# Dilated attention: three buffers for weight slices, scores left in PSUM until the exponential, output projection in eight chunks

## The chip, the cores and the metric

The kernel runs on one core of a Trainium2 chip. Five engines work from queues of their own and meet at semaphores: TensorE (PE) multiplies matrices and writes PSUM, VectorE (DVE) and ScalarE (ACT) do elementwise work and read and write PSUM and SBUF, GpSimd (POOL) works on SBUF alone, and SyncE (SP) issues most of the DMA transfers. SBUF is the working memory; PSUM has eight banks of 128 partitions by 512 fp32 values. The metric is the device time of one execution in microseconds (us), as the median of several runs.

## The reference, cut to what matters

Two layers work on 256 tokens of width 1024. Layer 0 has a pooling mixer, layer 1 the attention that is changed here; each is followed by a mixture of 64 experts. A condition vector `c` gives shift, scale and gate of every sub-layer through `ada_w`.

```
mod = silu(c) @ ada_w[i] + ada_b[i]                 # shift, scale, gate, twice
qkv = (h @ w_in).reshape(b, s, 3 groups, 3, 16 heads, 64)
for each group g (window, dilation) in ((128,1), (512,4), (2048,16)):
    sc = q @ k^T * 64**-0.5 - slope * distance      # only keys that are valid for g
    m = max(sc); p = exp(sc - m); den = sum(p)
    o_g = p @ v / den; lse_g = m + log(den)
mixed = sum_g softmax(lse)_g * o_g                  # (256, 16 heads * 64)
y = mixed @ w_out
x = layer_norm(ALPHA * x + (1 + g1) * y)            # then the experts of layer 1
```

The three groups of a head are the same as one softmax over all their keys together, and so the kernel computes them: 512 columns of scores (256 of group 0, 128 each of groups 1 and 2) for one query block.

## The kernel before

Everything is written out by hand for each engine in program order; there is no scheduler. The order of each engine's queue is the order of the Python code under `@block.sync`, `@block.scalar`, `@block.vector` and `@block.tensor`.

The attention layer is built like this:

- **Slices.** The input weight (1024 x 9216) arrives in 36 slices of 1 MB (`load_slice`), nine for each of four batches of heads; slices 36 to 39 are the output weight. To multiply fp32 data, each slice is split in two fp32r parts: ACT casts the high part (`slice_high`, line 780) and DVE subtracts it from the raw slice to get the low part (`slice_low`, line 445). Both parts lie in `slice_parts` (`wr`), which has two buffers. `project(n)` on PE is 48 matmuls of 256 columns (three products for each of 16 pieces, lines 1462 to 1464), and ACT copies its result out (`projected(n)`, line 808), then casts slice n+2.
- **Heads.** There are 16 steps that the code calls heads, `h` from 0 to 15, four to a batch (`HB`). One step is two real heads (index `j`) for one block of 128 queries. Per step: PE computes scores into banks 0 and 1 (`scores`, line 1525); DVE adds slope times distance, six instructions (line 1158), and takes the negative maximum, two (line 1163); ACT takes the exponential with its sum (line 824), DVE the reciprocal (line 1176), ACT multiplies (line 828); PE transposes the probabilities into banks 2 and 3 (line 1553); ACT and DVE copy one bank each to SBUF (`pT`, lines 832 and 1181); PE multiplies by the values (line 1564); DVE copies the 128 columns of result to `mixedT` (line 1192, `o_ready`).
- **What fills PE meanwhile.** `proj_of_head` puts projections of the next batch before and after the transposes of a step. The last batch has none; there `out_project(q)` for q = 0 to 3 (24 matmuls of 512 columns each) stands between the steps. It needs high and low parts of four heads' results, which ACT (`mixed_high`, line 814) and DVE (`mixed_low`, line 1169) make from `mixedT`.
- **Modulation.** The condition's matrix product runs beside this: DVE accumulates eight products for each 2 MB slice of `ada_w` (`gemv`, lines 865 and 867, in two halves, `part` 0 and 1), PE sums over partitions (`ada_sum`), DVE reads the sum (`ada_final`). Slices 16 to 23 belong here; they are loaded alternately into `slots0` ("S") and into units 6 and 7 of the weight memory.

Scores are biased from PSUM into the SBUF tile `sp_`, where the exponential also reads; so `scores(h+1)` waits on `s_read`, DVE's reading. DVE's list for a step begins with the reciprocal and the copy of `pT`, and only then has the bias and maximum of the next step.

Names for the text: S, T and V are the scores, transposes and value products on PE; P is one `project`.

Of the kernel before, what the change touches and what calls it, by code (L numbers as in the profile page):

```python
# [26 lines left out]
P = 128  # L27
# [12 lines left out]
HD = 64  # L40
# [88 lines left out]
def build(nc, a, out):  # L129
    ctx = ExitStack()  # L130
    with ctx:
# [106 lines left out]
        wr = in_weights("slice_parts", 0, [P, 2, 2, KD, BCOL], F32R)  # L238
# [11 lines left out]
        ada_place = [0, 2, 4, 6, "S", 0, 2, 4, 6, "S", "X", "S", 0, 2, 4, 6] + ["S", 6] * 4  # L250
# [17 lines left out]
        def sum_bank(n):  # L268

            return 5 if n >= 16 else (6, 7, 4, 5)[n - 12] if n >= 12 else 6 + n % 2  # L270
# [64 lines left out]
        s_mm, s_read, max_ready, p_exp, t_mm = sem("s_mm"), sem("s_read"), sem("max_ready"), sem("p_exp"), sem("p_T_mm")  # L335
# [36 lines left out]
        def proj_of_head(hb, hh):  # L372

            if hb == BATCHES - 1:
                return [], []
            before, after = [([0], [1]), ([2], [3]), ([4], [5]), ([6, 7], [8])][hh]
            return [9 * (hb + 1) + j for j in before], [9 * (hb + 1) + j for j in after]

# [4 lines left out]
        def gemv_of_head(hb, hh):  # L383

            return (18 + (hb * HB + hh) // 2, hh % 2) if hb < BATCHES - 1 else None

        def sum_of_head(hb, hh):

            return {(0, 1): 17, (0, 2): 18, (1, 0): 19, (1, 2): 20, (2, 0): 21, (2, 2): 22, (3, 0): 23}.get((hb, hh))
# [28 lines left out]

        def tokens_out(t, ks):

            return tmp[:, t, ks.start * P:ks.stop * P].rearrange("p (k r i) -> p k r i", k=4, r=4)
# [21 lines left out]
        def slice_lower(ops, n):  # L443

            ops.tensor_tensor(wr[:, n % 2, 1], slice_w(n), wr[:, n % 2, 0].bitcast(F32), ALU.subtract).then_inc(w_lo, 1)  # L445
# [3 lines left out]
        def _(sp):  # L449
# [96 lines left out]
            GEMV_LOADS = (12, 14, 17, 22, 26, 31)  # L546
# [21 lines left out]
            sp.wait_ge(ada_mm, 10)  # L568
            load_ada(17)
            for n in range(RAW, SLICES):  # L570
                if n in GEMV_LOADS:
                    m = 18 + GEMV_LOADS.index(n)
                    sp.wait_ge(ada_acc, m - 11)
                    load_ada(m)
                sp.wait_ge(w_lo, n - RAW + 1)
                load_slice(n)
# [87 lines left out]
        def _(act):  # L664
# [110 lines left out]
            def slice_high(n):  # L775
                if n < SLICES:
                    act.wait_ge(raw_in[n % RAW], 16 * (n // RAW + 1))
                    if n >= 2:
                        act.wait_ge(proj_mm, n - 1)
                    copy(wr[:, n % 2, 0], slice_w(n)).then_inc(w_hi, 1)  # L780
# [22 lines left out]
            slice_high(1)  # L803

            def projected(n):
# [4 lines left out]
                slice_high(n + 2)  # L810

            def mixed_high(b):

                copy(hThi[:, 2 * b:2 * b + 2], mixedT[:, 2 * b:2 * b + 2]).then_inc(hT_act, 1)

            for n in range(9):
                projected(n)
            for hb in range(BATCHES):
                for hh in range(HB):
                    h = hb * HB + hh  # L820
                    before, after = proj_of_head(hb, hh)
                    for j in range(2):
                        act.wait_ge(max_ready, 2 * h + j + 1)
                        nc.scalar.activation(sp_[:, j], sp_[:, j], ACT.Exp, bias=negmax[:, j:j + 1],
                                             accum_out=zsum[:, j:j + 1]).then_inc(p_exp, 1)
                    act.wait_ge(z_ready, h + 1)
                    for j in range(2):
                        nc.scalar.activation(sp_[:, j], sp_[:, j], ACT.Copy, scale=zinv[:, j:j + 1]).then_inc(p_ready, 1)
                    for n in before:
                        projected(n)  # L830
                    act.wait_ge(t_mm, h + 1)
                    copy(pT[:, 0], PS[:, 2, :]).then_inc(pT_act, 1)
                    if hb == BATCHES - 1 and hh < HB - 1:
                        mixed_high(hh)
                        if hh:
                            slice_high(9 * BATCHES + hh + 1)
                    for n in after:
                        projected(n)
            act.wait_ge(o_ready, HEADS)
            mixed_high(BATCHES - 1)  # L840
# [6 lines left out]
        def _(dve):  # L847
# [295 lines left out]
            for n in range(1, 11):  # L1143
                slice_low(n)
                if n in (6, 8):
                    gemv(16 + (n - 6) // 2, 0)
                if n in (7, 9):
                    gemv(16 + (n - 7) // 2, 1)
                if n == 10:
                    ada_final(16)  # L1150

            dve.wait_ge(dist_in, 16)
            def head_scores(h):
                hb, pair, it = place(h)
                dve.wait_ge(s_mm, h + 1)
                for j in range(2):
                    for g, (c0, c1) in enumerate(((0, 256), (256, 384), (384, 512))):
                        last = V.scalar_tensor_tensor(sp_[:, j, c0:c1], distT[:, it, c0:c1], -slope(g, hb * HB + 2 * pair + j),  # L1158
                                                      PS[:, j, c0:c1], ALU.mult, ALU.add)
                last.then_inc(s_read, 1)  # L1160
                dve.wait_ge(s_read, h + 1)
                for j in range(2):
                    V.tensor_reduce(negmax[:, j:j + 1], sp_[:, j], AX.X, ALU.max, negate=True).then_inc(max_ready, 1)
# [7 lines left out]
            head_scores(0)  # L1171
            for h in range(HEADS):
                hb, hh = h // HB, h % HB
                nxt = [n + 2 for part_of in proj_of_head(hb, hh) for n in part_of]
                dve.wait_ge(p_exp, 2 * (h + 1))
                V.reciprocal(zinv[:, :], zsum[:, :]).then_inc(z_ready, 1)
                early = nxt[:1] if hh == HB - 1 else []
                for n in early:
                    slice_low(n)
                dve.wait_ge(t_mm, h + 1)  # L1180
                copy(pT[:, 1], PS[:, 3, :]).then_inc(pT_dve, 1)
                if hh < HB - 1:
                    head_scores(h + 1)
                if (piece := gemv_of_head(hb, hh)) is not None:
                    gemv(*piece)
                if (n := sum_of_head(hb, hh)) is not None:
                    ada_final(n)
                for n in nxt[len(early):1]:
                    slice_low(n)
                dve.wait_ge(o_mm, h + 1)  # L1190
                _, pair, it = place(h)
                last = copy(in_order(mixedT, 2 * hb + pair)[:, 2 * it:2 * it + 2], PS[:, 2, 0:P].rearrange("p (r i) -> p r i", r=2))
                last.then_inc(o_ready, 1)
                for n in nxt[1:]:
                    if n < 9 * BATCHES:
                        slice_low(n)
                if hb == BATCHES - 1:
                    mixed_low(hh)
                    if hh < HB - 1:
                        slice_low(9 * BATCHES + hh + 1)  # L1200
                elif hh == HB - 1:
                    head_scores(h + 1)
                    if hb == BATCHES - 2:
                        slice_low(9 * BATCHES)
# [7 lines left out]
        def _(pe):  # L1212
# [105 lines left out]
            def moe(L):  # L1318
# [8 lines left out]
                pe.wait_ge(hT_act, (4, 14)[L])  # L1327
                pe.wait_ge(hT_dve, (4, 14)[L])
# [137 lines left out]
            def project(n):  # L1466
# [9 lines left out]
                w = wr[:, n % 2]  # L1476
# [11 lines left out]
            def out_project(q):  # L1488

# [145 lines left out]
```

## Time and profile before

| | |
|---|---|
| median of 3 runs | 1536.61 us (1533.97 to 1537.8) |
| profiled execution, its own time | 1533.0 us |
| its span, first to last instruction | 1531.2 us |
| mean granted TensorE clock | 0.976 of full |
| busy: PE / DVE / ACT / POOL | 1436.8 / 570.4 / 405.5 / 65.0 us |

The span has five parts: layer 0 with its experts (to about 630 us), the first nine projections (647.8 to 704.95), the 16 head steps (to 981.8, where the last output slice starts), norm and routing (to 1035.8), and the experts of layer 1. The profile's page gives busy shares over the whole span; the head steps are under a fifth of it, so what they wait for is read from views of that stretch alone. In a view of waits, "PE psum L1462 <- DVE slice_parts L445" means that PE stood idle before the instruction at line 1462 until the instruction of DVE at line 445 had ended. The granted clock is a share of full speed; 1.00 is 2.4 GHz, 0.50 is 1.2 GHz.

### The profile page before, as it was taken

The numbers are of one execution on the slowest core, as the hardware profiler recorded it, in microseconds if no ns is written. First come the engines' busy times: TensorE is split into PE (matmuls) and PEld (weight loads), VectorE is DVE, ScalarE is ACT, GpSimd is POOL, SyncE is SP. The second block draws the span as 40 slices with busy tenths as digits, with TensorE's granted clock in tenths as the row PEclk, the third lists the DMA queues.
The fourth block names the chain that finished last, engine by engine and source line by source line (L and its number), as shares of the span: only waits on it lengthen the run. The fifth ranks groups of instructions, "written<-read, shape, count | busy, mean of one in ns | idle before, by whom it ended". The sixth has DMA issues, their size and how long they took to land.

```text
span 1531.2 us, 19331 instructions
## 1 busy us (share of the span) xinstructions
PE 1436.8 (94%) x7546; PEld 818.7 (53%) x7546; DVE 570.4 (37%) x1108; ACT 405.5 (26%) x629; POOL 65.0 (4%) x46
## 2 busy tenths in 40 slices
PE   6999999999999999899888888689999999999994
PEld 3544444444444444498888887544444444444442
DVE  0574222222222222648566665551222222222225
ACT  1222112121221212435444444331212122121212
POOL 0001300000000000030000000022000000000001
PEclk9999999999999999899999999889999999999998
DMA  9994899999999999966444431367999999999990
GB/s 394 423 427 190 357 420 424 426 427 424 428 425 428 426 425 428 409 223 249 170 161 184 176 141 49 144 248 318 424 424 428 424 429 425 425 427 425 429 409 29
DMA packets 50512, 522.17 MB, mean 341 GB/s; under 512 B 5632, under 2 KB 5888, under 8 KB 8224
## 3 DMA queue, kind: packets, MB, share of 16 engines
q1 hardware_dynamic: 48512, 514.61, 80.9%
q0 software_dynamic: 1952, 6.88, 1.3%
q8 instruction: 34, 0.56, 0.1%
q14 instruction: 14, 0.11, 0.0%
HBM read 520.42 MB, written 1.05 MB: 341 GB/s over the span
## 4 chain that ended last, share of the span: by engine, by line
PE 87%; DVE 9%; DMA 2%; ACT 1%; issue 1%; SPq 0%; DVEq 0%; ACTq 0%
PE psum L1411 29%; PE psum L1436 15%; PE psum L1359 9%; PE psum L1368 9%; PE psum L1462 4%; PE psum L1463 4%; PE psum L1464 4%; PE psum L1267 2%; PE psum L1345 2%; PE psum L1312 2%; DVE slice_parts L445 2%; DVE modulation_sums L867 1%; DVE scores L1158 1%; PE psum L1553 1%; PE psum L1423 1%
## 5 line engine op out<-in xcount | busy, mean ns | idle before, releaser
L1411 PE MATMUL psum<-weights,slots_of_tokens 128*64 128x512 f32 x2048 | 450.4, 592 | 0.0
L1411 PEld LDWEIGHTS psum<-weights,slots_of_tokens 128*64 128x64 f32 x2048 | 146.9, 137 | 292.7 <-issue 292.7
L1436 PE MATMUL psum<-weights,hidden_T 128*64 128x512 f32 x1024 | 233.8, 598 | 0.0
L1112 DVE SCALAR_TENSOR_TENSOR slot_rows<-psum,slot_weight,slot_rows 128x512 fp32r<-128x512 f32 x128 | 96.1, 751 | 193.8 <-ACT slot_rows L770 193.8
L1098 DVE TENSOR_TENSOR hidden<-gate,psum 128x256 f32<-128x256 f32 x64 | 27.0, 421 | 374.8 <-ACT gate L762 374.8
L1359 PE MATMUL psum<-slot_matrix,h_parts 128*128 128x512 f32 x576 | 157.4, 399 | 0.0
L1368 PE MATMUL psum<-slot_rows,slots_T 128*128 128x512 f32 x528 | 140.5, 408 | 3.7 <-DVE slot_rows L1112 3.7
L1436 PEld LDWEIGHTS psum<-weights,hidden_T 128*64 128x64 f32 x1024 | 67.8, 136 | 132.8 <-issue 132.8
L1368 PEld LDWEIGHTS psum<-slot_rows,slots_T 128*128 128x128 f32 x528 | 94.6, 189 | 74.8 <-issue 57.3
L1462 PE MATMUL psum<-h_transposed_high,slice_parts 128*128 128x256 f32 x384 | 112.4, 293 | 23.0 <-DVE slice_parts L445 17.3
L762 ACT ACTIVATE gate<-psum 128x256 f32<-128x256 f32 x64 | 24.6, 384 | 410.2 <-PE psum L1411 410.2
L770 ACT ACTIVATE slot_rows<-psum,slot_weight 128x512 fp32r<-128x512 f32 x128 | 87.9, 687 | 136.3 <-PE psum L1436 136.3
L1359 PEld LDWEIGHTS psum<-slot_matrix,h_parts 128*128 128x128 f32 x576 | 103.6, 189 | 19.2 <-issue 1.0
L1463 PE MATMUL psum<-h_transposed_low,slice_parts 128*128 128x256 f32 x384 | 111.2, 290 | 0.0
L1464 PE MATMUL psum<-h_transposed_high,slice_parts 128*128 128x256 f32 x384 | 111.1, 289 | 0.0
L445 DVE TENSOR_TENSOR slice_parts<-weights,slice_parts 128x2048 fp32r<-128x2048 f32 x40 | 93.6, 2344 | 42.8 <-ACT slice_parts L780 42.7
L1462 PEld LDWEIGHTS psum<-h_transposed_high,slice_parts 128*128 128x128 f32 x384 | 76.3, 199 | 25.3 <-issue 24.3
L1100 DVE CAST slots_T<-psum 128x256 fp32r<-128x256 f32 x64 | 27.2, 425 | 161.3 <-PE psum L1425 161.3
L1462 PE MATMUL psum<-slice_parts,h_transposed_high 128*128 128x256 f32 (+1 forms) x224 | 69.2, 309 | 12.4 <-DVE slice_parts L445 6.4
L1464 PEld LDWEIGHTS psum<-h_transposed_high,slice_parts 128*128 128x128 f32 x384 | 76.3, 199 | 0.0
L1463 PEld LDWEIGHTS psum<-h_transposed_low,slice_parts 128*128 128x128 f32 x384 | 76.2, 198 | 0.0
L780 ACT CAST slice_parts<-weights 128x2048 fp32r<-128x2048 f32 x40 | 75.8, 1894 | 0.0
(182 smaller groups left out, 1386.6 us busy)
## 6 DMA issues: line engine op xcount, KB each, us to landing
weights<-in_exp_w_gu SPq DMA_DIRECT2D x128, 2048.0 KB, 15.6
weights<-in_exp_w_down SPq DMA_DIRECT2D x128, 1024.0 KB, 14.6
weights<-in_attn_w_in SPq DMA_DIRECT2D x36, 1024.0 KB, 6.1
weights<-in_ada_w SPq DMA_DIRECT2D x16, 2048.0 KB, 16.7
slots_of_tokens<-in_ada_w SPq DMA_DIRECT2D x7, 2048.0 KB, 13.0
weights<-in_pool_w_in SPq DMA_DIRECT2D x2, 2048.0 KB, 25.7
weights<-in_pool_w_out SPq DMA_DIRECT2D x2, 2048.0 KB, 20.5
weights<-in_sh_w_gu SPq DMA_DIRECT2D x2, 2048.0 KB, 10.1
```

The costliest lines, as they stand in the source:

```text
L445: ops.tensor_tensor(wr[:, n % 2, 1], slice_w(n), wr[:, n % 2, 0].bitcast(F32), ALU.subtract).then_inc(w_lo, 1)
L770: nc.scalar.activation(yw[:, 0, half * HALF:(half + 1) * HALF], PS[:, BD + half, :], ACT.Copy, scale=wslot[:, 0:1]).then_inc(lo.yh, 1)
L780: copy(wr[:, n % 2, 0], slice_w(n)).then_inc(w_hi, 1)
L1112: V.scalar_tensor_tensor(yw[:, 1, c], PS[:, BD + half, :], wslot[:, 0:1], yw[:, 0, c].bitcast(F32), ALU.mult, ALU.subtract).then_inc(lo.yl, 1)
L1267: last = mm(PS[:, u_bank(half, t), :], hT[:, k, t * P:(t + 1) * P], w_in[part][:, k - 4 * part, half * HALF:(half + 1) * HALF], start=k == ...
L1359: last = mm(PS[:, bank, :], hfs[:, s, t, k, :], Pm[b][:, t, :], start=s == 0 and t == 0, stop=s == 1 and t == TT - 1)
L1368: last = mm(PS[:, 2 * t + half, :], PT[:, t * P:(t + 1) * P], yw[:, s, half * HALF:(half + 1) * HALF], start=False, stop=True, skip_group_ ...
L1411: last = mm(PS[j * SLOTS:(j + 1) * SLOTS, BGU, :], XgT[ob][:, k, s0:s0 + SLOTS], gu_w(ws + j)[:, k, :], start=k == 0, stop=k == KD - 1, ti ...
L1436: last = mm(PS[j * SLOTS:(j + 1) * SLOTS, BD + half, :], HT[:, k, j * SLOTS:(j + 1) * SLOTS], dn_w(ws + j)[:, k, half * HALF:(half + 1) * ...
L1462: mm(out, *parts(0, 0), start=first, stop=False)
L1463: mm(out, *parts(1, 0), start=False, stop=False)
L1464: return mm(out, *parts(0, 1), start=False, stop=last)
```

## The change

- `slice_parts` gets a third buffer, in units 6 and 7. ACT casts slice n+3 after projection n, not n+2. Slices 0 to 2 are prepared ahead of the first projection.
- All modulation slices 16 to 23 are now loaded into `slots0`, each when the one before has been used (`GEMV_LOADS`, `ada_place`). Two of them, not one, are finished in the first nine projections; the others stand at the end of DVE's list of steps 0 to 9, then at steps 10 and 11. The last sum uses bank 3.
- DVE adds the bias in place, in PSUM, and takes the maximum there; the exponential reads PSUM and writes `sp_`. `scores(h+1)` now waits on `p_exp`, until ACT has read the scores of step h.
- DVE's list of a step begins with the bias and maximum of step h+1 (`head_scores(h + 1)`), ahead of the copy of `pT`; ACT's softmax of step h+1 stands behind its `pT` copy of step h and ahead of its `projected(after)`. At steps 3 and 7 (`scores_late`) the next step's scores come at the end, since they need the last projection.
- The projections of the last batch end at step 10 (three a step in steps 8 to 10), and `out_project` is cut in eight chunks of 12 matmuls: two each at steps 11, 12 and 13, one at 14, the last behind step 15.
- In steps 12 to 15 ACT and DVE write the high and low parts straight from PSUM, without `mixedT`.

```diff
-        wr = in_weights("slice_parts", 0, [P, 2, 2, KD, BCOL], F32R)
+        wr = [in_weights(f"slice_parts{i}", u0, [P, 2, KD, BCOL], F32R) for i, u0 in enumerate((0, 2, 6))]
-        ada_place = [0, 2, 4, 6, "S", 0, 2, 4, 6, "S", "X", "S", 0, 2, 4, 6] + ["S", 6] * 4
+        ada_place = [0, 2, 4, 6, "S", 0, 2, 4, 6, "S", "X", "S", 0, 2, 4, 6] + ["S"] * 8
+        def out_of_head(h):
+            return {HEADS - 5: (0, 1), HEADS - 4: (2, 3), HEADS - 3: (4, 5), HEADS - 2: (6,)}.get(h, ())
+        def sum_of_head(h):
+            return 17 + h // 2 if h % 2 == 0 and 2 <= h <= 10 else None
-            GEMV_LOADS = (12, 14, 17, 22, 26, 31)
+            GEMV_LOADS = (9, 13, 19, 24, 28, 33, 39)
...
@@ ACT @@
-                    for j in range(2):
-                        act.wait_ge(max_ready, 2 * h + j + 1)
-                        nc.scalar.activation(sp_[:, j], sp_[:, j], ACT.Exp, bias=negmax[:, j:j + 1],
...
+            softmax(0)
+            for h in range(HEADS):
+                for n in before:
+                    projected(n)
+                act.wait_ge(t_mm, h + 1)
+                copy(pT[:, 0], PS[:, 2, :]).then_inc(pT_act, 1)
+                if h < HEADS - 1 and not scores_late(h):
+                    softmax(h + 1)
+                for n in after:
+                    projected(n)
+                if scores_late(h):
+                    softmax(h + 1)
+                if h == HEADS - HB - 1:
+                    mixed_high(BATCHES - 2)
+                if h >= HEADS - HB:
+                    act.wait_ge(o_mm, h + 1)
+                    copy(o_in(hThi, h), o_out()).then_inc(hT_act, 1)
...
@@ DVE @@
-                        last = V.scalar_tensor_tensor(sp_[:, j, c0:c1], distT[:, it, c0:c1], -slope(g, hb * HB + 2 * pair + j),
+                        last = V.scalar_tensor_tensor(PS[:, j, c0:c1], distT[:, it, c0:c1], -slope(g, hb * HB + 2 * pair + j),
                                                       PS[:, j, c0:c1], ALU.mult, ALU.add)
-                    V.tensor_reduce(negmax[:, j:j + 1], sp_[:, j], AX.X, ALU.max, negate=True).then_inc(max_ready, 1)
+                    V.tensor_reduce(negmax[:, j:j + 1], PS[:, j, :], AX.X, ALU.max, negate=True).then_inc(max_ready, 1)
...
+                if early:
+                    head_scores(h + 1)
+                if (n := sum_of_head(h)) is not None:
+                    ada_final(n)
                 dve.wait_ge(t_mm, h + 1)
                 copy(pT[:, 1], PS[:, 3, :]).then_inc(pT_dve, 1)
+                if early:
+                    softmax_inverse(h + 1)
+                for n in before:
+                    slice_low(n + 3)
+                if h == HEADS - HB - 1:
+                    gemv(*gemv_of_head(h))
...
+                for n in after:
+                    slice_low(n + 3)
+                if gemv_of_head(h) is not None and h != HEADS - HB - 1:
+                    gemv(*gemv_of_head(h))
...
@@ PE @@
-                    pe.wait_ge(s_read, h)
+                    pe.wait_ge(p_exp, 2 * h)
```

**Place 1, DVE, step 1.** In these rows of the order `scores`/`psum` with `distances` is the bias, `slice_parts` the low part of a slice, `modulation_sums` a gemv half. Before:

```order
L1181 COPY probabilities_T<-psum 128x512
L1158 SCALAR_TENSOR_TENSOR scores<-distances,psum 128x256
L1158 SCALAR_TENSOR_TENSOR scores<-distances,psum 128x128 x2
L1158 SCALAR_TENSOR_TENSOR scores<-distances,psum 128x256
L1158 SCALAR_TENSOR_TENSOR scores<-distances,psum 128x128 x2
L1163 TENSOR_REDUCE negative_maximum<-scores 128x1 x2
L867 SCALAR_TENSOR_TENSOR modulation_sums<-slots_of_tokens,condition_silu,modulation_sums 128x512 x4
L884 SCALAR_TENSOR_TENSOR gates<-psum,gates 128x512
L445 TENSOR_TENSOR slice_parts<-weights,slice_parts 128x2048
L1192 COPY mixed_heads_T<-psum 128x2x64
L445 TENSOR_TENSOR slice_parts<-weights,slice_parts 128x2048
```

After, from the bias of step 2 to the end of the list of step 1:

```order
L1190 SCALAR_TENSOR_TENSOR psum<-distances,psum 128x256
L1190 SCALAR_TENSOR_TENSOR psum<-distances,psum 128x128 x2
L1190 SCALAR_TENSOR_TENSOR psum<-distances,psum 128x256
L1190 SCALAR_TENSOR_TENSOR psum<-distances,psum 128x128 x2
L1195 TENSOR_REDUCE negative_maximum<-psum 128x1 x2
L1218 COPY probabilities_T<-psum 128x512
L1200 RECIPROCAL softmax_inverse<-softmax_sum 128x2
L466 TENSOR_TENSOR slice_parts_82<-weights,slice_parts_82 128x2048
L1229 COPY mixed_heads_T<-psum 128x2x64
L466 TENSOR_TENSOR slice_parts_80<-weights,slice_parts_80 128x2048
L898 SCALAR_TENSOR_TENSOR modulation_sums<-slots_of_tokens,condition_silu,modulation_sums 128x512 x4
```

The bias and maximum have moved ahead of the `probabilities_T` copy, and the gemv half from the middle of the list to its end, behind both slices; PE's `ada_sum` of step 2 waits for that half.

**Place 2, DVE, where the output projection begins.** Before, step 12, which has no gemv:

```order
L1181 COPY probabilities_T<-psum 128x512
L1158 SCALAR_TENSOR_TENSOR scores<-distances,psum 128x256
L1158 SCALAR_TENSOR_TENSOR scores<-distances,psum 128x128 x2
L1158 SCALAR_TENSOR_TENSOR scores<-distances,psum 128x256
L1158 SCALAR_TENSOR_TENSOR scores<-distances,psum 128x128 x2
L1163 TENSOR_REDUCE negative_maximum<-scores 128x1 x2
L884 SCALAR_TENSOR_TENSOR gates<-psum,gates 128x512
L1192 COPY mixed_heads_T<-psum 128x2x64
L1169 TENSOR_TENSOR h_transposed_low<-mixed_heads_T,h_transposed_high 128x512
L445 TENSOR_TENSOR slice_parts<-weights,slice_parts 128x2048
```

After, the end of step 10 and most of step 11:

```order
L1206 TENSOR_TENSOR h_transposed_low<-mixed_heads_T,h_transposed_high 128x512 x2
L466 TENSOR_TENSOR slice_parts_82<-weights,slice_parts_82 128x2048
L896 TENSOR_SCALAR modulation_sums<-slots_of_tokens,condition_silu 128x512
L898 SCALAR_TENSOR_TENSOR modulation_sums<-slots_of_tokens,condition_silu,modulation_sums 128x512 x3
L1190 SCALAR_TENSOR_TENSOR psum<-distances,psum 128x256
L1190 SCALAR_TENSOR_TENSOR psum<-distances,psum 128x128 x2
L1190 SCALAR_TENSOR_TENSOR psum<-distances,psum 128x256
L1190 SCALAR_TENSOR_TENSOR psum<-distances,psum 128x128 x2
L1195 TENSOR_REDUCE negative_maximum<-psum 128x1 x2
L1218 COPY probabilities_T<-psum 128x512
L1200 RECIPROCAL softmax_inverse<-softmax_sum 128x2
L898 SCALAR_TENSOR_TENSOR modulation_sums<-slots_of_tokens,condition_silu,modulation_sums 128x512 x4
```

Both halves of the last gemv now stand here, the first ahead of the bias of step 12, the second ahead of the copy to `mixed_heads_T`.

**Place 3, PE, the end of the attention.** Before, the end of output slice 2, then step 15, then slice 3:

```order
L1463 MATMUL psum<-slice_parts,h_transposed_low 128x512
L1464 MATMUL psum<-slice_parts,h_transposed_high 128x512
L1553 MATMUL psum<-constants,scores 128x128 x8
L1564 MATMUL psum<-probabilities_T,qkv 64x128 x8
L1462 MATMUL psum<-slice_parts,h_transposed_high 128x512
L1463 MATMUL psum<-slice_parts,h_transposed_low 128x512
L1464 MATMUL psum<-slice_parts,h_transposed_high 128x512
L1462 MATMUL psum<-slice_parts,h_transposed_high 128x512
```

After, the end of chunk 6, the last `ada_sum`, V of step 14, then step 15 and chunk 7:

```order
L1505 MATMUL psum<-slice_parts_80,h_transposed_low 128x512
L1506 MATMUL psum<-slice_parts_80,h_transposed_high 128x512
L1278 MATMUL psum<-modulation_sums,constants 128x512
L1611 MATMUL psum<-probabilities_T,qkv 64x128 x8
L1594 MATMUL psum<-constants,scores 128x128 x8
L1611 MATMUL psum<-probabilities_T,qkv 64x128 x8
L1504 MATMUL psum<-slice_parts_80,h_transposed_high 128x512
L1505 MATMUL psum<-slice_parts_80,h_transposed_low 128x512
L1506 MATMUL psum<-slice_parts_80,h_transposed_high 128x512
```

The last sum stands between chunk 6 and V of step 14, and behind step 15 come 12 matmuls where there were 24.

## Rows read from the trace of the kernel before

**Rows 1.** The page: the chain that ended last, shares by engine.
```profile
PE 87%; DVE 9%; DMA 2%; ACT 1%; issue 1%; SPq 0%; DVEq 0%; ACTq 0%
```

**Rows 2.** Stretches: us from start, length, busy us of each engine, granted clock, DMA.
```profile
core 0: us, PE busy (x) PEld busy (x) DVE busy (x) ACT busy (x) POOL busy (x), PEclk, DMA share, GB/s
714.45:926.70 212.25, 188.61 (x1622) 181.32 (x1622) 129.81 (x202) 95.65 (x128) 0.00 (x0) 0.98 0.42 160
926.70:981.80 55.10, 41.45 (x283) 33.90 (x282) 30.98 (x59) 24.80 (x39) 0.54 (x1) 0.91 0.07 22
```

**Rows 3.** Waits from 714.4 to 981.8 us: total, times, longest.
```profile
PE psum L1462 <- DVE slice_parts L445: 23.6, 11, 2.7
...
PE psum L1462 <- DVE h_transposed_low L1169: 6.0, 4, 2.5
...
PE psum L1564 <- DVE probabilities_T L1181: 3.5, 4, 0.9
...
PE psum L1553 <- ACT scores L828: 3.3, 1, 3.3
```

**Rows 4.** Chain of waits through step 5: start us, length, instruction.
```profile
809.95 1.08 PE psum L1525 x12
811.03 1.04 PE psum L1553 x8
812.09 0.69 DVE probabilities_T L1181
812.78 1.46 DVE scores L1158 x6
814.27 1.28 DVE negative_maximum L1163 x2
815.55 0.67 DVE modulation_sums L867
...
818.57 2.21 DVE slice_parts L445
...
820.92 0.36 PE psum L1462
...
826.91 0.78 PE psum L1239 x8
```

**Rows 5.** Groups by line, 714.4 to 981.8 us: busy us, mean ns.
```profile
L780 ACT CAST slice_parts<-weights 128x2048 fp32r<-128x2048 f32 x29 | 54.9, 1893 | 0.0
...
L824 ACT ACTIVATE scores<-scores,negative_maximum 128x512 f32<-128x512 f32 x30 | 21.4, 715 | 15.0 <-DVE negative_maximum L1163 15.0
...
L1192 DVE COPY mixed_heads_T<-psum 128x128 f32<-128x128 f32 x16 | 6.2, 387 | 10.5 <-PE psum L1564 10.5
```

**Rows 6.** DMA issues into the block slots_of_tokens, 660 to 960 us.
```profile
DMA to landing us min/median/max: 7.9/7.9/8.8
```

**Rows 7.** Chain of waits from the second output slice to the next norm.
```profile
947.61 0.47 PE psum L1462
...
953.31 0.89 PE psum L1553 x8
...
977.90 0.70 DVE probabilities_T L1181
...
978.74 1.11 PE psum L1564 x16
...
980.28 0.63 ACT h_transposed_high L814
...
980.93 0.70 DVE h_transposed_low L1169
...
981.77 0.47 PE psum L1462
...
983.53 0.71 DVE psum L936
...
984.27 0.70 DVE residual_or_h L938
```

More of the change, by code:

```diff
@@ L1142, in _ @@
                     V.tensor_tensor(tokens_in(hTlo, ks, t), tokens_out(t, ks), tokens_in(hThi, ks, t).bitcast(F32), ALU.subtract).then_inc(hT_dve, 1)
-            for n in range(1, 11):
+            for n in range(1, 12):
                 slice_low(n)
[L1145 to L1149, printed above, removed]
+                if n in (3, 4):
+                    gemv(16, n - 3)
+                if n == 7:
                     ada_final(16)
+                if n in (7, 8):
+                    gemv(17, n - 7)
+            ada_final(17)
             dve.wait_ge(dist_in, 16)
@@ L1171, in _ @@
             head_scores(0)
+            softmax_inverse(0)
             for h in range(HEADS):
[L1173 to L1179, printed above, removed]
+                before, after = proj_of_head(h)
+                early = h < HEADS - 1 and not scores_late(h)
+                if early:
+                    head_scores(h + 1)
+                if (n := sum_of_head(h)) is not None:
+                    ada_final(n)
@@ L1192, in _ @@
[L1192 to L1204, printed above, removed]
+                if early:
+                    softmax_inverse(h + 1)
@@ L1569, in _ @@
-            out_project(BATCHES - 1)
+            for h in range(HEADS):
+                hb, pair, it = place(h)
+                before, after = proj_of_head(h)
+                for n in before:
+                    project(n)
+                n = sum_of_head(h)
+                if n is not None:
+                    ada_sum(n)
+                if h < HEADS - 1 and not scores_late(h):
+                    scores(h + 1)
+                if h:
+                    pe.wait_ge(pT_act, h)
+                    pe.wait_ge(pT_dve, h)
+                    pe.wait_ge(o_ready, h)
+                if h == HEADS - 1:
+                    pe.wait_ge(sum_read, ADA_SLICES)
+                for j in range(2):
+                    pe.wait_ge(p_ready, 2 * h + j + 1)
+                    for c in range(4):
+                        last = nc.tensor.transpose(PS[:, 2 + j, c * P:(c + 1) * P], sp_[:, j, c * P:(c + 1) * P], ident)
+                last.then_inc(t_mm, 1)
+                for n in after:
+                    project(n)
+                for c in out_of_head(h):
+                    if c == 0:
+                        pe.wait_ge(sum_read, ADA_SLICES - 1)
+                        pe.wait_ge(proj_copied, 9 * BATCHES)
+                    out_project(c)
+                pe.wait_ge(pT_act, h + 1)
+                pe.wait_ge(pT_dve, h + 1)
+                if h == HEADS - 2:
+                    ada_sum(ADA_SLICES - 1)
+                for c in range(4):
+                    for j in range(2):
+                        col = (0, 1, it, it)[c] * BCOL + (2 * pair + j) * HD
+                        v = qkv[:, hb % 2, (0, 0, 1, 2)[c], 2, col:col + HD]
+                        last = mm(PS[j * HD:(j + 1) * HD, 2, 0:P], v, pT[:, j, c * P:(c + 1) * P], start=c == 0, stop=c == 3,
+                                  tile_position=(0, j * HD))
+                last.then_inc(o_mm, 1)
+                if scores_late(h):
+                    scores(h + 1)
@@ L1570, in _ @@
+            out_project(KD - 1)
             moe(1)
```

185 lines of the change are left out of this document (82 added, 103 removed).

## The prediction

> **What bounds the kernel now.** I read the chain first: it runs 87% through PE and 9% through DVE [rows 1], so a gain has to come out of time in which PE stands still or runs slowly. The DVE part is the attention. The stretches show it: from 714.45 us (T of step 0 ends) to 926.70 (T of step 11 ends) PE is busy 188.61 of 212.25 us, in the last four steps 41.45 of 55.10 [rows 2]. DVE is busy 129.81 and ACT 95.65 of the first stretch, so neither is short of time. The waits name what is missing: 23.6 us in 11 waits for a low slice part, 6.0 in 4 for the low part of the mixed heads, 3.5 in 4 for the copy of pT, 3.3 in one for the softmax; 36.4 us in all [rows 3].
>
> One step shows the mechanism [rows 4]. S of step 6 ends at 811.03, T of step 5 at 812.07. Only now does DVE start: pT copy, bias, maximum, gemv half, then the low slice, to 820.78, 8.7 us after T. PE has one projection and V to fill this (817.7 us plus 1.1), and idles until 820.92. S was finished 1.0 us before T, but DVE's list had the pT copy first, and the slice that PE needed stood last, with only two buffers. So the bound is the order in DVE's list, not its load.
>
> The second loss is the clock. It was granted at 0.98 in the first stretch and 0.91 in the second [rows 2]; with levels of 2.4 and 1.2 GHz this is 8.5 and 9.9 us at the low one, of which half is lost: 4.2 + 5.0 = 9.2 us.
>
> **The change part by part.** All times are from the profiled execution (1533.0 us, span 1531.2). It is 3.6 us under the median of 1536.6, and I carry this difference over.
>
> *Slice waits.* With a third buffer the low part of slice n+3 is made while n+1 and n+2 wait ready, so project(n) is never late by DVE's list: a part may take two projections, 11.8 us (one is 5.9: 820.92 to 826.91 less its tail [rows 4]), and ACT's cast of 1.89 us [rows 5] plus DVE's 2.2 are far below. The 23.6 us go. So does the softmax wait of 3.3: bias and maximum of step h+1 start when S ends, 1.0 us before T ends, so from T's end they take to +1.8 us, pT copy +2.5, two exponentials of 0.9 with their sums +3.0, reciprocal, scaling +4.7. PE meanwhile has P, V and the next P: T of the next step is due at about +14.8. 10 us of slack.
>
> *What is late next: the gemv half.* It now stands behind the second slice of its step, and the sum of steps 2, 4, ... 10 needs the odd step's half. From the end of that step's last P: ACT copies the projection (0.6) and casts (1.9), DVE makes the low part (2.2 to 2.3) and the half (3.0: 815.55 to 818.57): 7.9 us. PE has V (1.1) and one P (5.8): 6.9 us. So PE waits 0.9 us at steps 2 and 6. At step 4 the late scores stand between: V and S (2.2 us), then bias and maximum (2.8), the exponentials (1.1 after the maximum's end) and the reciprocal, then slice (2.3) and half (3.0): 11.5 us against 2.2 + 5.8 = 8.0, a wait of 3.5. At step 8 and step 10 two projections precede the sum and hide it. Together 5.3 us. Behind the waiting sum stand S and T of the step, for which ACT and DVE wait in turn, but they have slack. The queue on SP is moved too: each 2 MB load now starts only when the half before is done, and lands after 7.9 to 8.8 us [rows 6]; the next half wants it 13.6 us later (a step of V 1.1, P 5.8, sum 0.8, S 1.1, T 1.0 and P 5.9, so 15.7, plus the wait of 0.9, less 7.9, plus the 4.9 us that copy, cast and low part take from P's end). Hidden.
>
> *The tail.* No projection stands in steps 11 to 15; two chunks, 5.7 us (947.61 to 953.31 [rows 7]), stand behind each T of 11 to 13. Counting from the end of the last P: DVE copies the mixed heads late (2.6, behind the two low slices of step 10), subtracts two pairs (4.0), slice 38 (6.2), half of the last gemv (9.1), bias and maximum of step 12 (11.9), pT copy of step 11 (12.6). PE is through V, S, T and both chunks at 9.7, so V waits 2.9 us. Then the second gemv half holds the copy of mixed heads (387 ns, [rows 5]) to 16.2, while PE has ended V and S at 14.8: T of step 12 waits 1.4. Behind: V(13) 0.3 (slice 39 ahead of the bias), T(14) 0.5 and T(15) 1.0 (the ACT copy and DVE subtraction of 0.4 each, behind the softmax), V(15) 0.9 as today (977.90 to 978.74), and chunk 7 1.0 where slice 3 waits 1.9 today (V's end 979.85 to 981.77). With 1.0 for T(11): 9.0 us. Before, this tail held 6.0 + 3.5 + 3.3 of the waits, so it gains little there.
>
> *The last chunk.* One more chunk comes ahead of the last one, +2.9 us. In return the first bank is done 3 matmuls after the start, not 6: the norm begins 0.9 us after chunk 7 starts, where it is 1.76 today (981.77 to 983.53 [rows 7]): −0.9.
>
> *PSUM instead of SBUF.* The trace shows no maximum over PSUM. From below: no change. From above: the 128x512 instruction that reads and writes PSUM in place took 0.71 us, one that writes SBUF 0.70, so 0.03 per instruction at most. Even 0.5 us per step would lie under the 10 us of slack in steps 0 to 10 and add 2.5 us in the tail; I take 0 and keep 2.5. The exponential (715 ns from SBUF) I leave as it is. The Trainium skill ("VectorE: DVE Perf Modes", section on the TRN2 errata) gives VectorE a higher fixed cost for a PSUM source than for an SBUF one, 120 against 58 cycles. By that estimate two maxima cost 0.13 us more, 0.7 us over the tail.
>
> *The rest.* The sum moved into the first nine projections costs there what it saves later. Norm and MoE are untouched: the experts' loads start when the output projection ends, as before, and all of it shifts with it.
>
> *The clock.* In the trace 37 us of waits brought 9.2 us of loss; 14.3 us at the same ratio bring 3.5. The Trainium skill ("TensorE: Matmul & The Clock Gate", "What's actually happening") says that an idle TensorE falls back to half its clock and must be busy before it gets it back; the trace agrees, since the stretch with more waits per time has 0.91. By the rule the 3.5 us wait of step 4 is the likeliest place.
>
> *Sum.* −36.4 − 9.2 − 0.9 + 2.9 + 5.3 + 9.0 + 3.5 = −25.8 us, so 1507.2 in a profiled execution and 1510.8 by the median; about 1510.
>
> **Rivals.**
> *R1: the sums don't wait and the tail is smooth.* If my reading of DVE's list is too slow and most of the 14.3 us of waits with their 3.5 of clock are absent, some 12 of these 17.8 us come back: 1498. For it: DVE has 82 us to spare in 212. Against: the order puts the half last.
> *R2: the gain is lost in the clock or in the tail.* If TensorE is at half clock in as much time as before although its waits are shorter (+5.7), and the in-place bias costs its bound (+2.5): 1519. For it: the last stretch, where waits stay, has the lowest clock. Against: 25 us of regular waits leave the first stretch.
> *R3, slower: the single block for modulation weights.* If a 2 MB load that must share the queue with 1 MB slices lands late, DVE stops at the half, PE at the sum. It costs nothing up to 13.6 us. Six loads (18 to 23) have to make up 25.8 us, so each must be 4.3 us beyond this: from 17.9 us on the kernel is slower; at 19, 6 x 5.4 = 32 us, 1543. Against: 8.8 at most in these steps. For it: the loads' neighbours in the queue are now packed closer.
> *R4: the change doesn't do what it says*, because ACT's cast of slice n+3 ahead of its pT copy holds the softmax, and PE waits 2.2 us a step as now: 11 x 2.2 = 24 us come back: 1535. Against: ACT has 10 us of slack a step.
>
> **How the numbers follow.** Forecast 0.62, R1 0.14, R2 0.16, R3 0.04, R4 0.04. The forecast's own range is 1503 to 1516 (the waits of 14.3 us by half, the PSUM bound). The range that holds the time 8 times in 10 takes in most of R1 and R2: 1497 to 1521. What can be told from no change is 0.3%, 4.6 us. Faster takes the forecast, R1 and R2, 0.92; R4 gives the 0.04 of same; R3 gives 0.04 of slower.
>
> **What would show it.** Right: PE's waits for slice_parts gone in steps 1 to 10; waits of 0.9, 3.5 and 0.9 us before the sums of steps 2, 4 and 6 put down to modulation_sums; from T of step 0 to T of step 11 about 199 us instead of 212; from there to chunk 7 42 us, where it is 55. The granted clock of the first stretch 0.99 or more. Wrong: waits for modulation_sums at all steps (R3), waits before T for the softmax (R4), or no wait at the sums (R1).

## The result, and the profile after

| | before | changed |
|---|---|---|
| median | 1535.29 us (4 runs, 1531.81 to 1537.8) | 1510.19 us (4 runs, 1507.74 to 1512.83) |
| profiled execution | 1533.0 us | 1507.74 us |
| span | 1531.2 us | 1506.0 us |

The ratio is 0.9838, with an interval from 0.981 to 0.9867: 25 us faster, against a forecast of 1510 and a gain of 25.8 us. The span is 25.2 us shorter. (A later measurement of the changed kernel, below, has one execution of 6517 us among its six; its median is 1508.21 us with it and 1508.19 without.) Where the gain came from is read in the same two stretches as [rows 2]: from the end of T of step 0 to that of step 11, and from there to the last output matmuls.

```profile
core 0: us, PE busy (x) PEld busy (x) DVE busy (x) ACT busy (x) POOL busy (x), PEclk, DMA share, GB/s
713.80:912.65 198.85, 193.55 (x1679) 186.27 (x1679) 131.12 (x197) 100.92 (x132) 0.00 (x0) 0.98 0.49 181
912.65:956.38 43.73, 35.67 (x235) 28.27 (x234) 28.19 (x58) 18.50 (x37) 0.00 (x0) 0.92 0.00 0
```

The first stretch fell from 212.25 to 198.85 us although it now holds one projection more (5.9 us): DVE does about the same work (131 us, was 130), ACT some more (101, was 96), and PE has 5 us without work where it had 24. The second fell from 55.10 to 43.73. It lost the moved projection (5.9) and took on one chunk (2.9); PE has 8 us without work where it had 14.

The waits of PE in the changed kernel, to set beside [rows 3] (total, times and longest in us, from 713.8 to 956.4 us):

```profile
PE psum L1281 <- DVE modulation_sums L898: 5.0, 3, 3.3
...
PE psum L1611 <- DVE probabilities_T L1218: 4.4, 3, 3.3
...
PE psum L1594 <- DVE h_transposed_low L1232: 1.7, 2, 1.1
PE psum L1504 <- DVE h_transposed_low L1232: 1.1, 1, 1.1
PE psum L1594 <- DVE mixed_heads_T L1229: 1.0, 2, 0.8
```

The 23.6 us for slice_parts are gone. New is the first row, the sums that wait for a gemv half. The chain through step 1 shows it as [rows 4] showed the old wait (start, length, instruction):

```profile
734.90 1.90 ACT slice_parts L799
736.83 2.29 DVE slice_parts L466
739.12 0.67 DVE modulation_sums L898
739.82 0.76 DVE modulation_sums L898
740.60 0.76 DVE modulation_sums L898
741.39 0.76 DVE modulation_sums L898
742.20 1.05 PE psum L1281 x8
743.25 1.08 PE psum L1570 x12
744.33 1.02 PE psum L1594 x8
```

From the end of the projection (734.3) ACT casts, DVE makes the low part and then the half, to 742.15, 7.8 us; PE had V and one projection and idled 0.85 us. The softmax of step 2 was ready long before T: DVE's list, bias first, then pT copy and reciprocal, ended this part at 731.68.

```profile
727.72 1.55 DVE L1190 SCALAR_TENSOR_TENSOR psum<-distances,psum 128x256 f32<-128x256 f32 x6 [0.67 <-PE psum L1570]
729.31 1.29 DVE L1195 TENSOR_REDUCE negative_maximum<-psum 128x1 f32<-128x512 f32 x2
730.51 0.68 DVE L1218 COPY probabilities_T<-psum 128x512 f32<-128x512 f32 x1
731.51 0.17 DVE L1200 RECIPROCAL softmax_inverse<-softmax_sum 128x2 f32<-128x2 f32 x1 [0.32 <-ACT scores L844]
731.60 2.27 DVE L466 TENSOR_TENSOR slice_parts<-weights,slice_parts 128x2048 fp32r<-128x2048 f32 x1
```

### The profile page after: what moved, and what is told of

Read it like the earlier page. It is cut to its first block, busy times and chain, and to the rows that moved or that the text cites. A ratio compares the mean times of both kernels' runs of the same rounds, so it can differ in the third digit from the quotient of the medians.

```text
span 1506.0 us, 19343 instructions
## 1 busy us (share of the span) xinstructions
PE 1433.3 (95%) x7546; PEld 815.9 (54%) x7546; DVE 576.7 (38%) x1107; ACT 406.5 (27%) x632; POOL 63.6 (4%) x46
## 3 DMA queue, kind: packets, MB, share of 16 engines
HBM read 520.42 MB, written 1.05 MB: 346 GB/s over the span
## 4 chain that ended last, share of the span: by engine, by line
PE 89%; DVE 5%; ACT 2%; DMA 2%; issue 1%; SPq 0%; DVEq 0%; ACTq 0%
PE psum L1453 29%; PE psum L1478 15%; PE psum L1401 9%; PE psum L1410 9%; PE psum L1504 5%; PE psum L1505 4%; PE psum L1506 4%; PE psum L1309 2%; PE psum L1387 2%; PE psum L1354 2%; PE psum L1594 1%; PE psum L1465 1%; DMA weights<-in_ada_w 1%; PE psum L1432 1%; DMA weights<-in_sh_w_down 1%
## 5 line engine op out<-in xcount | busy, mean ns | idle before, releaser
L1131 DVE CAST slots_T<-psum 128x256 fp32r<-128x256 f32 x64 | 27.2, 425 | 161.3 <-PE psum L1467 161.3
L783 ACT COPY hidden_T<-psum 128x256 f32<-128x256 f32 x64 | 23.8, 373 | 190.3 <-PE psum L1467 190.3
## 6 DMA issues: line engine op xcount, KB each, us to landing
weights<-in_pool_w_out SPq DMA_DIRECT2D x2, 2048.0 KB, 20.4
```

## The experiments

The changed kernel was measured three times: its medians were 1510.19, 1506.71 and 1508.21 us, its spans 1506.0, 1504.2 and 1504.3 us. The second belongs beside e5, e6 and e7, the third beside e8 and the second measurement of e6; e1 to e4 have only the kernel before beside them, so their distance from the changed kernel is given against both spans, 1506.0 and 1504.2. All ratios below are to the kernel before. "Loss" by the clock is half of the time at half clock, without the part in which PE was waiting anyway.

| edit | median us | ratio (interval) | span us |
|---|---|---|---|
| e3: changed, two buffers | 1546.84 | 1.0065 (1.0038 to 1.0092) | 1545.2 |
| e4: changed, pT copy ahead of the bias | 1518.47 | 0.9879 (0.9851 to 0.9907) | 1517.0 |
| e7: before, gemv half later | 1518.72 | 0.9883 (0.9857 to 0.9909) | 1516.9 |
| e1: changed, gemv half ahead of the low parts | 1501.06 | 0.9776 (0.975 to 0.9801) | 1499.1 |
| e2: changed, no gemv in steps 10 and 11 | 1502.23 | 0.9782 (0.9756 to 0.9807) | 1501.3 |
| e6: e1 and e2 together | 1493.48 | 0.9726 (0.97 to 0.9752) | 1492.9 |
| e5: changed, two chunks behind step 15 | 1510.71 | 0.9837 (0.981 to 0.9865) | 1508.9 |
| e8: changed, later loads | 1512.23 | 0.9854 (0.9828 to 0.988) | 1509.5 |

**e3, without the third buffer.**

```diff
-                    if n >= 3:
-                        act.wait_ge(proj_mm, n - 2)
-                    copy(wr[n % 3][:, 0], slice_w(n)).then_inc(w_hi, 1)
+                    if n >= 2:
+                        act.wait_ge(proj_mm, n - 1)
+                    copy(wr[n % 2][:, 0], slice_w(n)).then_inc(w_hi, 1)
...
-                slice_high(n + 3)
+                slice_high(n + 2)
...
```

> The changed kernel with two buffers of slice parts again (cast of slice n+2 behind projection n), all else as changed; slice 38 is split at step 11. Theory A (the third buffer is what lets DVE's order be as it is where three projections fall in a step): the low part for the projection behind T is made only behind the pT copy, so PE waits for slice_parts 3.0 us at steps 3 and 7 and 5.7 us at steps 8, 9 and 10, none in the steps with two projections; 23 us more and 5 to 8 us of clock: span 1534 to 1538. Theory B (the order of DVE's list alone removed the waits, the buffer is spare): at most 3 us more, 1509. Theory C (waits come back at every step, about 2 us each as before): 11 x 2.2 = 24 us more, spread evenly.

```profile
PE psum L1505 <- DVE slice_parts L466: 22.9, 6, 5.5
PE psum L1282 <- DVE modulation_sums L898: 5.0, 3, 3.3
```

Five waits stand where theory A put them, in front of the projection behind T: 3.14 at steps 3 and 7, 5.32, 5.39 and 5.50 at steps 8, 9 and 10; the sixth is one of 0.40 later in step 7, and the steps with two projections have none. Yet the span is 41 us over the changed kernel's 1504.2. All waits of PE sum to 36.7 us, 23.5 more than in the changed kernel's first profile, and the granted clock over the 282 us is 0.91, which is 51 us at half clock. Some 9 of these fell inside PE's waits, so about 21 us are lost, where the changed kernel loses 5 to 6.5. The clock adds 14 to 16 us to 23.5 of waits; I had expected 5 to 8.

**e4, the old order of pT copy and bias.**

```diff
-                if early:
-                    head_scores(h + 1)
-                if (n := sum_of_head(h)) is not None:
-                    ada_final(n)
                 dve.wait_ge(t_mm, h + 1)
                 copy(pT[:, 1], PS[:, 3, :]).then_inc(pT_dve, 1)
+                if early:
+                    head_scores(h + 1)
+                if (n := sum_of_head(h)) is not None:
+                    ada_final(n)
```

> The changed kernel with DVE's copy of pT ahead of the bias and maximum of the next step again; three buffers and PSUM scores stay. Theory A (with three buffers nothing waits for that order; from T's end the softmax needs 6.6 us and the next T is due at 14.8): no new wait in steps 1 to 10; at step 11 V waits about 0.5 us where it waits 3.3, but T(12) or S(13) about 3 us more; span 1504 to 1508. Theory B (the bound of the kernel before was this order, as the prediction's first part says): about 2 us a step come back as waits for the softmax or the slice, 1525 or more.

```profile
PE psum L1281 <- DVE modulation_sums L898: 5.3, 3, 3.3
PE psum L1594 <- DVE mixed_heads_T L1229: 4.3, 2, 2.6
PE psum L1594 <- DVE h_transposed_low L1232: 3.7, 2, 2.3
PE psum L1570 <- ACT scores L844: 2.5, 1, 2.5
...
PE psum L1504 <- DVE slice_parts L466: 0.4, 2, 0.2
```

In steps 1 to 10 theory A holds: no wait for the softmax comes back, the sums wait 0.1 us longer, slice parts 0.4 in all. V of step 11 no longer waits. But the tail, which has no projections to hide behind, pays: T of step 11 waits 1.78 us where it waited 0.26, S of step 13 2.48 for the exponential of step 12, T of step 12 2.56, T of steps 14 and 15 1.38 and 2.29 us. Together the waits grow by 5 us against the changed kernel's first profile, and the loss by the clock (23 us at half clock) by 3.5 to 5. 1517 is outside the 1504 to 1508 that I gave: the order is worth under 1 us of waits in the steps with projections, 6 to 8 us from there to chunk 7, and another 2 to 3 behind chunk 7, where half clock lasts longer (24.9 us, where the changed kernel has 17 to 20.5).

**e7, the kernel before with only the gemv half moved.**

```diff
                 V.reciprocal(zinv[:, :], zsum[:, :]).then_inc(z_ready, 1)
+                if hh and (piece := gemv_of_head(hb, hh - 1)) is not None:
+                    gemv(*piece)
...
-                if (piece := gemv_of_head(hb, hh)) is not None:
+                if hh == HB - 1 and (piece := gemv_of_head(hb, hh)) is not None:
```

> The kernel before with one edit: in steps 0 to 2 of each batch of four, DVE makes the gemv half behind the reciprocal of the next step, so that the first low part stands right behind the maximum. Two buffers, scores in SBUF. Theory A (the low part was late because 3.0 us of gemv stood ahead of it): 9 of the 11 waits for slice_parts (20.3 us) go, waits of about 1 us appear at the sums of steps 2, 6 and 10; with 3 us of clock the span falls by 20 us to 1511. Theory B (two buffers are the bound): the waits stay, 1528 or more. Theory C (the softmax is late instead, as the bias still waits for the pT copy): waits of 1 to 2 us before T, 1518 to 1522.

```profile
PE psum L1555 <- ACT scores L828: 3.3, 1, 3.3
PE psum L1464 <- DVE slice_parts L445: 3.3, 2, 1.6
PE psum L1241 <- DVE modulation_sums L867: 1.8, 2, 0.9
PE psum L1238 <- DVE modulation_sums L867: 0.9, 1, 0.9
```

Nine of the eleven slice waits are gone, with two buffers and the scores in SBUF; the two that stay are at steps 3 and 7, where the low part already stood first. Waits of 0.91 us came at the three sums, as expected. Span 1516.9, 14.3 us less; I had 20. The waits fell by 18 us, but the low clock gave back 3.4: through the last output slice 27.2 us at half clock, where before had 20.4. So 3 us of gemv ahead of the low part was the cause of nine of the eleven old waits. In the changed kernel the steps with two projections are cured twice over: e3 has the late half without the third buffer, e1 below has the buffer with the half ahead of the low parts, and neither waits for slice_parts there. The steps with three projections need the buffer (e3).

**e1 and e2, the two new waits.** e1 makes the gemv half ahead of the low parts in steps 0 to 9. e2 makes slices 22 and 23 whole at the end of steps 8 and 9, so steps 10 and 11 have none.

```diff
@@ e1 @@
                 if early:
                     softmax_inverse(h + 1)
+                if gemv_of_head(h) is not None and h < HEADS - HB - 2:
+                    gemv(*gemv_of_head(h))
...
-                if gemv_of_head(h) is not None and h != HEADS - HB - 1:
+                if h == HEADS - HB - 2:
                     gemv(*gemv_of_head(h))
@@ e2 @@
-            GEMV_LOADS = (9, 13, 19, 24, 28, 33, 39)
+            GEMV_LOADS = (9, 13, 19, 24, 28, 33, 36)
...
-                if h == HEADS - HB - 1:
-                    gemv(*gemv_of_head(h))
...
-                if gemv_of_head(h) is not None and h != HEADS - HB - 1:
-                    gemv(*gemv_of_head(h))
+                if h < 8:
+                    gemv(*gemv_of_head(h))
+                elif h < 10:
+                    gemv(14 + h)
```

> The changed kernel with one edit: in steps 0 to 9 DVE makes the gemv half right behind the reciprocal, ahead of the low parts, not at the end of its list. Theory A (the three waits of 0.85, 3.33 and 0.85 us before the sums of steps 2, 4 and 6 come from the place of the half in DVE's list, and the 6.8 us of half clock behind the longest of them from that wait): the three waits go to 0, the clock stays at full speed through steps 1 to 10, span 1506.0 - 5.0 - 3.4 = 1497.6 us. Theory B (the half took slack that the low parts need): waits of PE for slice_parts of 1 us or more appear in several steps, 1503 us or more. Theory C (the waits go but the low clock comes as it likes): 1501.

> The changed kernel with the last two modulation slices done whole at the end of steps 8 and 9 (slice 23 loaded one step earlier), so that steps 10 and 11 have no gemv half. Theory A: V of step 11 loses its wait of 3.30 us and T of step 12 its 0.76, and with them the 6.8 us of half clock behind: 4 + 3.4 us less, span 1498.5 us; no new wait in steps 8 to 10, where two projections hide 3 us more of DVE. Theory B (steps 8 to 10 have no room on DVE for 3 us more): PE waits before the scores or the sum there, gain under 3 us. Theory C (the bound moves to the copy of mixed heads and the softmax): V(11) waits 0 but S(13) or T(12) take 2 us of it, 1502.

e1 first, then e2:

```profile
PE psum L1613 <- DVE probabilities_T L1218: 4.4, 3, 3.3
PE psum L1506 <- DVE slice_parts L466: 3.0, 2, 1.6
```

```profile
PE psum L1281 <- DVE modulation_sums L898: 5.0, 3, 3.3
...
PE psum L1611 <- DVE probabilities_T L1218: 1.5, 3, 0.9
```

In e1 the three waits at the sums are gone and the clock is full from 713.5 to 900 us, but at steps 8 and 9, which have three projections, the half now holds the slices: 1.44 and 1.56 us, theory B in part. In e2 V of step 11 waits 0.41 instead of 3.30, T of step 12 not at all. e1 took 6.9 us off the first profile's 1506.0 (5.1 off 1504.2), e2 4.7 (2.9), not the 8.4 and 7.5 expected. Against the first profile the clock gave back about the 3.4 us that I had set for it, up to chunk 7, in both. What fell short in e1 is the 3.0 us of new slice waits. In e2 half clock lasts 3.4 us further into the stretch behind chunk 7, which took 1.3 us more, and the attention began 0.6 us later. The second profile had lost less by the clock to begin with, so there was less to win.

**e6, both.** Halves ahead of the low parts in steps 0 to 7, slices 22 and 23 at the end of steps 8 and 9, where e1's new waits were.

> The changed kernel with both edits: gemv halves ahead of the low parts in steps 0 to 7, slices 22 and 23 whole at the end of steps 8 and 9. If the two waits and the two stretches of half clock are independent: 8.4 + 7.5 us less than the changed kernel, span about 1490. If the low clock appears elsewhere instead: 1494 to 1497.

> The kernel with both edits once more, on the chip and beside the runs of the changed kernel: span 1491 to 1493, no wait of PE over 0.3 us from step 1 to step 10, and no stretch at half clock there if these need a wait of PE.

```profile
PE psum L1594 <- DVE h_transposed_low L1232: 1.7, 2, 1.1
PE psum L1611 <- DVE probabilities_T L1218: 1.5, 3, 0.9
PE psum L1504 <- DVE h_transposed_low L1232: 1.0, 1, 1.0
PE psum L1594 <- DVE mixed_heads_T L1229: 0.3, 1, 0.3
```

From step 1 to step 10 PE waits for nothing. Two measurements: 1493.48 and 1492.65 us (ratios 0.9726 and 0.9728, the second from 0.9702 to 0.9754). This version beats both kernels: 42 us under the kernel before, 13 to 16 under the changed one measured beside it. From step 0 its clock is full until 938.6 in one profile, 947.5 in the other.

**e5, one chunk more behind step 15.** `out_of_head` loses chunk 6 and `out_project(KD - 2)` is called ahead of the last.

> The changed kernel with chunk 6 moved behind step 15, so that chunks 6 and 7 both follow it. Theory A (a chunk of 2.86 us in step 14 covers the softmax of step 15 in part, and one behind step 15 lies wholly on the path): chunk 6 covers V(14)'s wait for pT (2.5 us) and the softmax, so little of step 14 shrinks; 2 to 3 us more, span 1508.5. Theory B (step 14 is bound by PE): the step shrinks by the chunk and the span stays, 1506.

4.7 us over the span of the changed kernel measured beside it (1508.9 against 1504.2), the medians 4.0 apart. At step 14 PE waits 2.15 us ahead of the sum, where chunk 6 had filled the time:

```profile
PE psum L1278 <- issue: 2.2, 1, 2.2
```

The profile names no releaser; the wait ends 0.1 us after DVE's pT copy has read bank 3 (947.87 us), which the last sum uses. So nearly the whole chunk of 2.9 us is on the path, as in theory A; the rest comes with two stretches of 3.4 us at half clock, at 948.2 and 955.1 us. The chunk ahead of step 15 was thus a real part of the gain.

**e8, loads two weight slices later.** `GEMV_LOADS = (9, 13, 21, 26, 30, 35, 39)`.

> The changed kernel with the loads of modulation slices 19 to 22 two weight slices later in the queue, so each is issued about 8 us later and lands about 16 us after the half before it ended, where the next half wants it after 13.6 us. Theory A (the prediction's rival R3: DVE stops at the half and PE at the sum): waits of PE for modulation_sums grow by 2 to 3 us at steps 4 and 6, and scores or softmax waits appear; 5 to 8 us more, span 1511 or more. Theory B (a late first half only delays the next bias, which has 10 us of slack up to T, while the sum waits for the second half): DVE idles 2 to 3 us at the end of steps 2, 4 and 6, no wait of PE changes by more than 0.3 us, span as the changed kernel's, 1504 to 1507.

```profile
DVE modulation_sums L896 <- DMA slots_of_tokens<-in_ada_w: 17.1, 4, 5.9
PE psum L1281 <- DVE modulation_sums L898: 6.5, 3, 3.3
PE psum L1611 <- DVE probabilities_T L1218: 4.7, 4, 3.3
```

DVE idled 17.1 us in four waits, more than planned, and PE's waits grew by 1.8 us: 0.31 at V of step 5, 1.5 at the sum of step 6 (T of step 12 waited 0.9 less). The span grew by 5 us against 1504.3, some 3 of them by the clock: 17 us at half clock before chunk 7, where the changed kernel beside it had 10. Neither theory holds whole: in waits a late load costs PE about a tenth of what it costs DVE, not one for one as my rival R3 had it, but the clock comes on top.

**The changed kernel again.**

> The changed kernel again, beside the others on one chip: 1506 us span; waits of 0.85, 3.33, 0.85 before the sums and 3.30 before V of step 11 if they are fixed by the order, and the two stretches of 6.8 us at half clock behind the two waits of 3.3 us if these cause them.

> The changed kernel a third time, beside the two others: the same waits before the sums and before V of step 11; whether the low clock follows the wait of 0.85 us at step 2 (as in one of its two profiled executions) or not (as in the other).

The waits repeat to 0.02 us but one (T of step 12: 0.77, 1.73, 1.73; in the first profile V and S ahead of it ran at half clock and ended 1 us later). The low clock does not. The first profile had 6.8 us from 782.4 and 6.8 from 922.4, each behind a wait of 3.3 us; the other two had 3.4 us at 742.8, 783.8 and 817.9, behind the waits at the sums, the 0.85 ones too, and none behind the wait of 3.3 us at step 11. The same stretch in the first profile and the second:

```profile
742.90:746.30 3.40, 3.40 (x34) 3.22 (x34) 1.89 (x7) 1.45 (x2) 0.00 (x0) 1.00 0.94 304
```

```profile
742.90:746.30 3.40, 3.40 (x23) 3.18 (x20) 2.49 (x8) 0.62 (x2) 0.00 (x0) 0.51 0.91 366
```

PE is busy in both, behind the same wait of 0.85 us, but at 2.4 GHz in one and 1.2 GHz in the other.

## Why the prediction was right, and which steps of it were not

- *Slice waits, 23.6 us.* Right in size. The working put them down to the third buffer; e7 shows that the two buffers were not the cause of nine of the eleven, e3 that the steps with three projections need the third.
- *"The bound is the order in DVE's list, not its load."* Right, but one half of what I named did nothing. The gemv half ahead of the low part was the cause (e7, 14 us by one moved call). The pT copy ahead of the bias was not, in steps with projections (e4, and e7, which keeps it); from the tail on the new order is worth 8 to 11 us, which my part on the tail did not price.
- *The gemv half at the sums: 0.9, 3.5, 0.9.* Measured 0.85, 3.33, 0.85; none at steps 8 and 10. Removed by e1.
- *The tail, 9.0 us of waits.* Measured 8.2: V(11) 3.30 (2.9 forecast), T(12) 0.77 (1.4), T(11) 0.26 (1.0), V(13) 0.25, T(14) 0.56, T(15) 1.12, V(15) 0.88, chunk 7 1.05. That the last gemv slice caused V(11) and T(12), 4.1 of the 8.2, is shown by e2; the others stay there. The stretches came out at 198.85 and 43.73 us, forecast 199 and 42.
- *The clock, 3.5 us by the ratio of loss to waits.* The term that was mis-sized. Before chunk 7 the first profile had 13.6 us at half clock, half of it 6.8; the other two had 10.2, half of it 5.1. The 9.2 us for the kernel before was small too: it came from the rounded shares 0.98 and 0.91, and the profile has 20.4 us at half clock, half of it 10.2. So the clock gave back 3.4 us in the first profile and 5.1 in the others, where I had 5.7. A fixed share of the waits is no model: 37.3 us of waits came with 20.4 us at half clock in the kernel before, 36.7 with 51 in e3, where seven waits are of 3.1 us or more (in the kernel before, one). Half clock followed the wait of 3.3 us at step 4 in all three profiles, as I expected, but in two of them the waits of 0.85 as well. My sign of "0.99 or more" in the first stretch failed (0.98); without waits, in e1 and e6, it is 1.00 from 713.5 to 900 us.
- *The last chunk, −0.9 us in front of the norm.* Chunk 7 ran at half clock in the first profile (3.4 us from 956.5), so the norm began 1.66 us after its start, almost the 1.76 of before. In the second profile, at full clock, it was 1.07, still over 0.9.
- *The sum.* That −25.8 met the measured −25.2 so closely is in part luck, for the errors cancel. In the first profile the clock lost 3.3 us more than forecast, and the stretch from chunk 7 on gave nothing for the forecast 0.9. Against these stand 1.0 that the old clock had cost beyond 9.2, 0.9 for two old waits of S for the bias (scores L1158) that I left out of the 36.4, 1.1 less in the new waits, and T of step 0, which ended 0.65 us earlier.
- *PSUM instead of SBUF.* The exponential gained, and DVE lost almost nothing:

```profile
L844 ACT ACTIVATE scores<-psum,negative_maximum 128x512 f32<-128x512 f32 x30 | 20.4, 685 | 20.4 <-DVE negative_maximum L1195 20.4
...
L1195 DVE TENSOR_REDUCE negative_maximum<-psum 128x1 f32<-128x512 f32 x30 | 19.3, 685 | 0.5
```

  The maximum took 681 ns from SBUF and 685 from PSUM. The 62 cycles between a PSUM and an SBUF source in the Trainium skill's page "VectorE: DVE Perf Modes" (section on the TRN2 errata), 65 ns each as an estimate at the 0.96 GHz given there, are not seen; the measurement decides. The exponential fell from 715 ns [rows 5] to 685. No run keeps the scores in SBUF with all else as changed, nor the copy to `mixedT` in steps 12 to 15, so what these two parts gave is not shown.
- *Rivals.* R1 (no waits at the sums) did not happen by itself; e6 shows what it is worth, 13 to 16 us, with half of the tail's waits gone too. R2 names the clock, which did lose more than forecast, by 1.6 to 3.3 us, not 5.7. R3 did not occur, loads landed in 7.8 to 8.9 us, and its price was wrong (e8). R4 did not occur.

## What to carry to other kernels

Write down each engine's list for one step with durations and ask, for each item that another engine waits for, what stands ahead of it. Work that nobody waits for soon belongs behind work that someone does, and moving it needs no memory. When it moves to the end of a list, look who waits for the end: here a sum, for 5 us, and a tail without cover. Judge an order separately where there is work to hide behind and where there is none. And price a wait of PE above its length, since half clock may follow it: in e3 23.5 us of added waits cost 41 us.

## What the runs showed of the hardware

- Behind a wait of PE the granted clock dropped in some executions to 1.2 GHz for 3.4 or 6.8 us, even behind one of 0.85; whether it did differs between executions with waits equal to 0.02 us (the first profile of the changed kernel against the other two). The largest part of e3's loss beyond its waits is this.
- DVE read and wrote one PSUM bank in place nearly as fast as it read PSUM and wrote SBUF: the bias took 425 ns against 413 (256 columns) and 289 against 281 (128).
- A DMA of 2 MB landed in 7.6 to 8.9 us with 1 MB slices between (changed kernel, three profiles). It took up to 10.8 with later loads (e8) and up to 11.3 in e1, whose loads stand at the same places in the queue as the changed kernel's.
